# Query stage, head and last projection of a hybrid encoder kernel put in another order

## What is computed

```python
for layer in range(2):
    g = norm_gains[layer]
    h = h + 0.5 * rms_norm(swiglu(rms_norm(h, g[0]), ffn_w_in[layer, 0], ffn_w_out[layer, 0]), g[1])
    hn = rms_norm(h, g[2])
    m = attention_mixer(...) if layer == 0 else recurrent_mixer(...)
    h = h + rms_norm(m, g[3])
    h = h + 0.5 * rms_norm(swiglu(rms_norm(h, g[4]), ffn_w_in[layer, 1], ffn_w_out[layer, 1]), g[5])
return h[:, 16:]          # swiglu(x) = (silu(x @ w_in[:, :2816]) * (x @ w_in[:, 2816:])) @ w_out
# attention: q and k are RMS-normed per head of 64, rotated, q scaled by 1/8; 16 query heads, 4 key heads
```

## Time and profile before

| | |
|---|---|
| median of three executions | 1121.16 us |
| the profiled execution | 1124.99 us |
| its span, first to last instruction | 1123.2 us |
| mean granted TensorE clock | 0.987 of full |
| TensorE busy | 1074.9 us (96%), 8696 matmuls |
| VectorE, ScalarE, GpSimd busy | 716.9, 552.4, 117.7 us |
| read from HBM | 167.30 MB, 150 GB/s over the span |
| chain that ended last | TensorE 85%, VectorE 11% |

### The profile page before, as it was taken

How to read it: one execution, slowest core, us unless ns; L and a number is a source line. 1 busy time by engine, 2 the same in 40 slices (tenths; PEclk the granted TensorE clock), 3 DMA queues, 4 the chain that set the end, 5 groups by cost and what they waited for, 6 DMA issues and landing times.

```text
span 1123.2 us, 21352 instructions
## 1 busy us (share of the span) xinstructions
PE 1074.9 (96%) x8696; PEld 1046.3 (93%) x8696; DVE 716.9 (64%) x1012; ACT 552.4 (49%) x806; POOL 117.7 (10%) x103
## 2 busy tenths in 40 slices
PE   6999999998899999999999999999997699999998
PEld 5999999987669999999999999999897699999997
DVE  5766655475574766664467666545889967666542
ACT  4544454452575544435454534534587455444541
POOL 2000000033100200000020000000477310000000
PEclk9999999998999999999999999999998899999999
DMA  8565446625103255445645454557153163645541
GB/s 245 192 202 169 133 148 201 230 76 160 39 1 113 82 193 176 150 155 169 211 141 187 152 173 154 162 185 225 56 171 125 33 217 125 214 153 174 179 131 38
DMA packets 166464, 169.65 MB, mean 151 GB/s; under 512 B 3312, under 2 KB 165416, under 8 KB 166392
## 3 DMA queue, kind: packets, MB, share of 16 engines
q1 hardware_dynamic: 166088, 168.16, 46.6%
q0 software_dynamic: 96, 0.28, 0.1%
q10 hardware_dynamic: 208, 0.20, 0.1%
HBM read 167.30 MB, written 1.05 MB: 150 GB/s over the span
## 4 chain that ended last, share of the span: by engine, by line
PE 85%; DVE 11%; issue 2%; ACT 2%; DMA 1%; POOL 0%; SPq 0%; DVEq 0%
PE bank L365 25%; PE bank L367 24%; PE bank L366 24%; DVE wl L1090 2%; DVE h L1133 1%; PE bank L393 1%; PE flipped L582 1%; DVE gm L1386 1%; PE weighed L594 1%; DVE mg L1129 1%; DVE xl L1096 1%; PE bank L373 1%; ACT wh L735 1%; PE bank L486 1%; PE bank L384 1%
## 5 line engine op out<-in xcount | busy, mean ns | idle before, releaser
L1090 DVE TENSOR_TENSOR wl<-raw,wh 128x2048 fp32r<-128x2048 f32 (+2 forms) x178 | 366.3, 2078 | 177.2 <-ACT wh L735 176.8
L365 PE MATMUL bank<-xh,wl 128*128 128x272 f32 (+1 forms) x1552 | 451.1, 291 | 10.4 <-DVE xl L1391 7.9
L367 PE MATMUL bank<-xh,wh 128*128 128x272 f32 (+1 forms) x1552 | 448.4, 289 | 0.0
L366 PE MATMUL bank<-xl,wh 128*128 128x272 f32 (+1 forms) x1552 | 446.9, 288 | 0.0
L735 ACT ACTIVATE wh<-raw 128x2048 fp32r<-128x2048 f32 (+2 forms) x177 | 299.3, 1714 | 97.3 <-PE bank L367 97.3
L365 PEld LDWEIGHTS bank<-xh,wl 128*128 128x128 f32 x1552 | 295.4, 190 | 13.0 <-DVE xl L1391 8.1
L366 PEld LDWEIGHTS bank<-xl,wh 128*128 128x128 f32 x1552 | 295.3, 190 | 0.1
L367 PEld LDWEIGHTS bank<-xh,wh 128*128 128x128 f32 x1552 | 295.3, 190 | 0.0
L365 PE MATMUL bank<-ah,wl 128*128 128x272 f32 (+1 forms) x704 | 201.5, 286 | 0.0
L367 PE MATMUL bank<-ah,wh 128*128 128x272 f32 (+1 forms) x704 | 201.1, 286 | 0.0
L366 PE MATMUL bank<-al,wh 128*128 128x272 f32 (+1 forms) x704 | 201.1, 286 | 0.0
(11 more groups left out here) (165 smaller groups left out, 1145.2 us busy)
## 6 DMA issues: line engine op xcount, KB each, us to landing
raw<-in_ffn_w_in SPq DMA_DIRECT2D x88, 1024.0 KB, 5.2
raw<-in_ffn_w_out SPq DMA_DIRECT2D x32, 768.0 KB, 5.1
raw<-in_ffn_w_out SPq DMA_DIRECT2D x32, 640.0 KB, 4.3
raw<-in_rec_w_in SPq DMA_DIRECT2D x8, 1024.0 KB, 5.4
raw<-in_attn_w_qkv SPq DMA_DIRECT2D x6, 1024.0 KB, 5.0
raw<-in_attn_w_o SPq DMA_DIRECT2D x4, 1024.0 KB, 5.2
raw<-in_rec_gate_w SPq DMA_DIRECT2D x16, 256.0 KB, 3.7
raw<-in_rec_w_out SPq DMA_DIRECT2D x4, 1024.0 KB, 5.7
```

The costliest lines, as they stand in the source:

```text
L365: pe.matmul(dst, b, mh, start=first, stop=False)
L366: pe.matmul(dst, a, ml, start=False, stop=False)
L367: return pe.matmul(dst, a, mh, start=False, stop=last)
L1090: dve.tensor_tensor(wl[:, slot(u), 0:kn * 256], w, wh[:, slot(u), 0:kn * 256].bitcast(F32), ALU.subtract).then_inc(w_ready, 1)
```

## The change

*Head.* The tokens' last rows are loaded by SP and the norm vectors by ScalarE's queue, instead of the other way round. TensorE starts with 22 warming products on a zeroed tile (`WARM`), turns the first chunk of tokens, then the norm vectors, then the other chunks. Units 0 and 1 are split by halves (`high_half`, `low_half`); the gate tiles use the first half of unit 0 before the second is there, and all high parts of x before the low ones (`first_tiles`). The low parts of x chunks 6 and 7 are made by GpSimd.

*Means behind projections.* Three warming products of each `mean_of_projection` are gone.

*Keys, values, queries.* The key and value products with x's high part stand ahead of the wait for its low part. In a query tile the means and the rotation of the tile before stand after chunk 3, and its spread at the tile's end; VectorE makes a tile's factor at once, behind its sine part.

*Last projection.* The hidden tokens are held still (128 at a time) and 512 columns of the output weights are moved, so the output has tokens on the partitions. Twelve weight units of up to 4 x 512 columns (`LAST_K`) replace sixteen. h is turned earlier, in four groups between the FFN's tiles (`turn_h`), and copied by ScalarE into `h_tok`. The norm's squares are summed along the row by ScalarE; gain, factor and residual are applied to rows of 512. The gain is broadcast by a DMA to all partitions.

```diff
+XL_DVE = 6
+WARM = 22
...
+            def last_out(vout):
+                sp.wait_ge(pv_done, 2 * NKV)
+                sp.wait_ge(xr_done, KC)
+                sp.dma_start(last_gain, gains[1, 5:6, :].broadcast_to([P, D])).then_inc(s_gain, 16)
+                for half in range(2):
+                    for j, kn in enumerate(LAST_K):
+                        u = U_LAST + len(LAST_K) * half + j
+                        sp.wait_ge(w_ready, u - WEIGHT_SLOTS + 1)
+                        dst = raw[:, slot(u), 0:kn * 512].rearrange("p (k c) -> p k c", k=kn)
+                        sp.dma_start(dst, vout[:, 4 * j:4 * j + kn, 512 * half:512 * half + 512]).then_inc(landed[slot(u)], 16)
...
-            def chunk(tiles, k, norm, t0):
+            def chunk(tiles, k, norm, t0, values=None, done=None):
                 pe.wait_ge(xh_ready, KC * norm + k + 1)
...
                     a, b = (v[:, slot(u), tile * P:(tile + 1) * P] for v in (wh, wl))
                     pe.matmul(dst, b, xh[:, k, t0:L], start=k == 0, stop=False)
                     pe.matmul(dst, a, xh[:, k, t0:L], start=False, stop=False)
+                if values is not None:
+                    x, wv_h, wv_l, parts = values
+                    for dst, a in parts:
+                        pe.matmul(dst, x[:, k, a:a + KT], wv_l, start=k == 0, stop=False)
+                        pe.matmul(dst, x[:, k, a:a + KT], wv_h, start=False, stop=False)
                 pe.wait_ge(x_ready, KC * norm + k + 1)
-                return [pe.matmul(dst, wh[:, slot(u), tile * P:(tile + 1) * P], xl[:, k, t0:L], start=False, stop=k == KC - 1)
+                last = [pe.matmul(dst, wh[:, slot(u), tile * P:(tile + 1) * P], xl[:, k, t0:L], start=False, stop=k == KC - 1)
                         for dst, u, tile in tiles]
+                if done is not None and k == KC - 1:
+                    for product_done in last:
+                        product_done.then_inc(done, 1)
+                return last
+            def first_tiles(tiles):
+                for k in range(KC):
+                    if k % 4 == 0:
+                        pe.wait_ge(w_ready if k else w_half, 1)
+                    pe.wait_ge(xh_ready, k + 1)
+                    for dst, u, m in tiles:
+                        a, b = (v[:, slot(u), (2 * k + m) * P:(2 * k + m + 1) * P] for v in (wh, wl))
+                        pe.matmul(dst, b, xh[:, k, :], start=k == 0, stop=False)
+                        pe.matmul(dst, a, xh[:, k, :], start=False, stop=False)
+                for k in range(KC):
+                    if k < XL_DVE:
+                        pe.wait_ge(x_ready, k + 1)
+                    else:
+                        pe.wait_ge(xl_pool, k - XL_DVE + 1)
+                    for dst, u, m in tiles:
+                        pe.matmul(dst, wh[:, slot(u), (2 * k + m) * P:(2 * k + m + 1) * P], xl[:, k, :], start=False, stop=k == KC - 1)
...
-                keep_warm(3, bank[5])
...
+            def turn_h(i):
+                t, half = divmod(i, 2)
+                if i:
+                    pe.wait_ge(h_turned_copied, i)
+                for c in range(4):
+                    last = pe.transpose(bank[6][:, c * P:(c + 1) * P], h[:, 4 * half + c, META + t * P:META + (t + 1) * P], ident)
+                last.then_inc(h_turned, 1)
+            def last_out(f0):
+                def rows(half, t, j, k):
+                    f, u = 4 * j + k, U_LAST + len(LAST_K) * half + j
+                    if half == 0 and t == 0:
+                        pe.wait_ge(a_ready, f0 + f + 1)
+                    dst = last_bank(half, t)[:, :]
+                    th, tl = (v[:, f, META + t * P:META + (t + 1) * P] for v in (ah, al))
+                    h512, l512 = (v[:, slot(u), 512 * k:512 * k + 512] for v in (wh, wl))
+                    pe.matmul(dst, th, l512, start=f == 0, stop=False)
+                    pe.matmul(dst, tl, h512, start=False, stop=False)
+                    return pe.matmul(dst, th, h512, start=False, stop=f == FC - 1)
+                n = len(LAST_K)
+                for half in range(2):
+                    for j in range(n - 1 - half):
+                        pe.wait_ge(w_ready, U_LAST + n * half + j + 1)
+                        for k in range(LAST_K[j]):
+                            for t in range(2):
+                                last = rows(half, t, j, k)
+                        last.then_inc(last_unit_used, 1)
+                    pe.wait_ge(w_ready, U_LAST + n * half + n)
+                    for t in range(2):
+                        for j in range(n - 1 - half, n):
+                            for k in range(LAST_K[j]):
+                                last = rows(half, t, j, k)
+                        last.then_inc(y_done, 1)
...
+                    chunk([(bank[m][:, 0:L], U_QKV, 2 * k + m) for m in range(KT_N)], k, 1, 0, (xh, wv_h, wv_l, values), qk_done)
+                    for dst, a in values:
+                        last = pe.matmul(dst, xl[:, k, a:a + KT], wv_h, start=False, stop=k == KC - 1)
...
-                        if t == KT_N and k == 2:
+                        if t == KT_N and k == 1:
                             pe.wait_ge(v_ready, 3)
                             head_means(0)
                             rotate(0)
-                        if k == 4:
+                        if k == 3:
                             head_means(t - 1)
                             rotate(t - 1)
-                            if t > KT_N:
-                                spread_scale(t - 2)
-                        if t == QKT - 1 and k == 4:
+                        if t == QKT - 1 and k == 5:
                             pe.wait_ge(k_dup, 32)
                             scores(0)
                     last.then_inc(qk_done, 1)
                     if t == KT_N:
                         spread_scale(0)
+                    spread_scale(t - 1)
...
+            pe.wait_ge(pad_zero, 1)
+            for _ in range(WARM):
+                pe.matmul(bank[0][:, 0:P], pad[:, 0, 0:P], pad[:, 0, 0:P], start=True, stop=True)
+            pe.wait_ge(s_in, 16)
             pe.wait_ge(s_xin, 64)
             for c in range(KC):
                 if c >= 4:
                     pe.wait_ge(h_ready, c - 3)
-                elif c == 0:
-                    pe.wait_ge(vec_ready, 2)
                 for t, (a, n) in enumerate(TOK):
                     last = pe.transpose(bank[4 + c % 4][:, a:a + n], tok_in[0:n, t, c * P:(c + 1) * P], ident[0:n, 0:n])
                 last.then_inc(x_trans, 1)
-            keep_warm(16, bank[0])
+                if c == 0:
+                    pe.wait_ge(s_vin, 16)
+                    pe.transpose(bank[3][:, 0:96], vrow[:, 0, :], ident[0:96, 0:96]).then_inc(vecs_t, 1)
+            keep_warm(4, bank[1])
...
+            def copy_h(i):
+                t, half = divmod(i, 2)
+                act.wait_ge(h_turned, i + 1)
+                act.activation(h_tok[:, t, 512 * half:512 * half + 512], bank[6][:, :], ACT.Copy).then_inc(h_turned_copied, 1)
+            def last_out():
+                load_table(ACT.Sqrt)
+                for i in range(5):
+                    high(U_LAST + 4 + i, 0, KC, (last_unit_used, i + 1))
+                def squares(half, t):
+                    act.wait_ge(y_done, 2 * half + t + 1)
+                    if half + t:
+                        act.wait_ge(y_squared, 2 * half + t)
+                    act.activation(junk, last_bank(half, t)[:, :], ACT.Square, accum_out=ysq[:, t, half:half + 1]).then_inc(y_squared, 1)
+                high(U_LAST + 9, 0, KC, (y_done, 2))
+                squares(0, 0)
+                squares(0, 1)
+                high(U_LAST + 10, 0, KC, (last_unit_used, 6))
+                high(U_LAST + 11, 0, 2 * LAST_K[-1], (last_unit_used, 7))
+                for t in range(2):
+                    squares(1, t)
+                    act.wait_ge(y_sum, t + 1)
+                    act.wait_ge(y_squared, 3 + t)
+                    act.activation(yrt[:, t, 1:2], ysq[:, t, 1:2], ACT.Sqrt, scale=4.0 / D, bias=yrt[:, t, 0:1]).then_inc(y_root, 1)
...
+            for c in range(3):
+                x_high(0, c)
+            high_half(0, 0)
+            x_high(0, 3)
+            x_high(0, 4)
+            high_half(0, 1)
+            for c in range(5, KC):
+                x_high(0, c)
+            high_half(1, 0)
+            high_half(1, 1)
...
+                for i in range(6):
+                    low(U_LAST + 4 + i, 0)
+                for t in range(2):
+                    dve.wait_ge(y_squared, t + 1)
+                    dve.tensor_scalar(yrt[:, t, 0:1], ysq[:, t, 0:1], 4.0 / D, 4.0 * EPS, ALU.mult, ALU.add).then_inc(y_sum, 1)
+                    gained(0, t)
+                low(U_LAST + 10, 0)
+                low(U_LAST + 11, 0, 2 * LAST_K[-1])
+                dve.wait_ge(h_turned_copied, 4)
+                for t in range(2):
+                    gained(1, t)
+                    dve.wait_ge(y_root, t + 1)
```

(39 more changed lines are left out.)

180 lines of the change are left out of this document (98 added, 82 removed).

## The result

Over 8 runs each, the changed kernel took 1116.24 us in the median (1111.36 to 1118.91) and the kernel before 1121.74 (1120.13 to 1124.85). The ratio is 0.9946, 95% interval 0.9929 to 0.9963: 6.1 us faster (4.1 to 8.0). Forecast was 1106.0 with a range of 1101 to 1112. The sign was right; the size was wrong, and the median lies outside the range.

What follows compares the result with a forecast made beforehand. TensorE was busy 96% of the span, so only gaps, side work and low-clock stretches could yield time. 3.3 + 0.75 + 2.6 + 4.2 + 0.3 - 2.3 + 6.3 = 15.2 us off the 1121.16 median gave 1106.0, range 1101 to 1112.

Steps and rivals of the forecast that it cites:

- head: Start of the kernel: earlier warming, turning and half splits bring the first product on unit 2 forward, 3.3 us gained (1.5 to 4.5).
- three warming products fewer, five times: Means behind the five projections: the spread starts 0.15 us earlier each time, 0.75 us gained (0 to 1).
- query stage, order: Keys, values and queries: the new order of TensorE's and VectorE's work gains 2.6 us (1.5 to 4).
- query stage, clock: Query stage: two low-clock stretches behind factor waits disappear, 4.2 us gained (0 to 4.2).
- last projection: Last projection: 264 products of 512 columns replace 528 of 256, 61.9 us instead of 62.2, 0.3 gained.
- turning h: 16 turnings move from the tail into TensorE's full stretch: 2.3 us lost (2.1 to 4.5).
- tail: After the last product's start: 6.5 us to the end of the span instead of 12.85, 6.3 gained (5.3 to 7).
- Rival 1: Clock still falls in the query stage, at the values wait, or in the head before first products: 1110.2 us; chance 0.25.
- the closing 1.3: End of the query stage: after the last tile a spread (0.8) and a squares wait (0.5) fall together, 1.3 us gained.
- rival 2: Last projection: products carry a fixed cost each, so 512 columns take 224.5 ns; 2.6 us more gained, 1103.4; chance 0.10.
- Rivals 3 and 4: 3: head gives 1.0 us or less, 1108.5, chance 0.09; 4: last projection's weight loads no longer hidden, 1180, chance 0.04.

## Why the prediction was wrong, step by step

| step | predicted | what the runs showed |
|---|---|---|
| head | 3.3 | 0 as made [-1.5, 1.0]; 3.0 [1.7, 4.3] with the wait behind it filled |
| three warming products fewer, five times | 0.75 | -1.3 [-2.7, -0.1] |
| query stage, order | 2.6 | 1.4 (0.6 ahead of the mean of h, 0.75 behind it) |
| query stage, clock | 4.2 | 3.0 to 4.2 in the stage, but order and clock together 2.0 [0.6, 3.5] |
| last projection | 0.3 | 1.2 |
| turning h | -2.3 | -1.7 |
| tail | 6.3 | 7.0 |

By their ratios, the parts alone give 0 - 1.3 + 2.0 + 6.5 = 7.2, which agrees with the 6.1 (4.1 to 8.0) of the whole. Where no interval stands, the figure comes from one or a few profiles.

**The step that failed is the clock**: "The new waits are 1.2, 1.2, 0.9 and one of 1.8, so I take the stretches as gone: 4.2." That the old ones go was right. That the new waits are harmless was not: at the one for the values (1.8 in the prediction, 1.2 in the trace) the clock fell (244.07 to 250.90), and at the head's, which I had worked out myself as a pause between 28 and 31.7, it fell as well. The term's bounds, 0 and 4.2, left no room for stretches that were not there before, and the 3.3 of the head and the 0.75 of the means had no price for the clock at all. I took a single row, the 1.8 us wait at 806.5, for a rule, against the rows of 2.4 us beside it; in the changed kernel the same wait has a low stretch behind it at 803.86. One row at 1.00 shows that the clock can stay, not that it does. Rival 1 had 0.25 and named the wait for the values; in the head it named the place between turning and first products, where the clock stayed up, and not the wait for unit 2. It priced the matter as 4.2 not gained, 1110.2, though the new stretches stood ready to take back the gain of the head besides.

**"With this cover gone the next thing late is the reciprocal itself"** was the second: the cost of taking warming products out was counted in their 0.15 us, not in what they are for. The spread does start 0.15 earlier (2.07 behind the mean's start, before 2.22), as worked out. But the earlier trace rows shows a chain of small products with no gap; without the three it has a gap of 0.46, and a low stretch followed in five of five means with them alone taken out, in three of five in the changed kernel.

**The order of the query stage** was followed rightly tile by tile up to the end (times from the query stage alone, against the old order with its waits filled): tile 1's rotation is 2.2 later than in the old order with a warm clock (predicted 2.1), tile 2's 1.6 (1.5), and the tiles with the old waits take 6.0 and 6.3 us in place of 7.3, 1.3 and 1.0 gained (1.4 each). Two things were over-counted: 0.3 more lost in the tile before, and the closing 1.3, of which the first turned tile shows 0.15.

**Right:** the tail, step by step (last start to end 5.8 for 6.5: the 3.04 behind the last copy became 2.5 behind the last result), and the head's start; the first product on unit 2 came at 30.39, for 31.7. A product of 512 columns is 231.6 ns: 2.9 below my line through 256 and 272 columns (234.5), 7.1 above the 224.5 of rival 2. Rivals 3 and 4 did not come about either: the clock was up when the tokens were turned, and the products became no slower. The Trainium skill, "TensorE: Matmul & The Clock Gate", section "Wait — 56ns, not 53.3ns?", would put it, as an estimate, at 512/2.4 + 2.5 = 216; the trace doesn't agree, as it did not at 256. GpSimd's scaling of one part of x took 1.26 and 1.16 us where I had 0.79; the sum began at 18.94 all the same. One reading was loose: the 197 ns of the old head's warming records are a mean, 213 ns up to 21.4 us and 112 from 21.6 on, so the clock rose within them and not behind them.

The profiled run of before, 3.2 us above its median in the later runs, made no error by itself, since I subtracted from the median. But it was an unlucky one: the clock rose late in its head, and its query stage lost 4.2 where three other profiles lost 3.0. And it made this low clock look like a loss that ends with its cause.
